# Expert stage laid out anew: 8 KB weight rows into four banks, the second matrix one job behind, low halves over the raw part, row tables ahead of the loop

## The reference

```
h = RMSNorm(x);  logits = h @ w_router + b_router
gate = softmax(top 4 of logits)
gu  = h_rows @ w_gu[e] + b_gu[e]                     # 1024 -> 2048 (gate | linear)
g   = min(gu[:, :1024], 7);  l = clip(gu[:, 1024:], -7, 7)
act = g * sigmoid(1.702 * g) * (l + 1)
y   = act @ w_down[e] + b_down[e]                    # 1024 -> 1024
x[token] += gate * y      for each of the token's four experts
```

## Time and profile before

| | us |
|---|---|
| median of 3 runs | 1790.51 (1790.03 to 1791.18) |
| the profiled execution, its own time | 1789.55 |
| its span, first to last instruction | 1787.7 |
| PE busy, whole span | 1642.5 (92%) |
| DVE busy | 1384.4 (77%) |
| ACT busy | 1089.3 (61%) |
| POOL busy | 235.4 (13%) |
| mean granted PE clock | 0.98 |

### The profile page before, as it was taken

How to read it: one execution, slowest core, us unless ns; L and a number is a source line. 1 busy time by engine, 2 the same in 40 slices (tenths; PEclk the granted TensorE clock), 3 DMA queues, 4 the chain that set the end, 5 groups by cost and what they waited for, 6 DMA issues and landing times.

```text
span 1787.7 us, 23152 instructions
## 1 busy us (share of the span) xinstructions
PE 1642.5 (92%) x7877; PEld 1203.5 (67%) x7877; DVE 1384.4 (77%) x1531; ACT 1089.3 (61%) x1073; POOL 235.4 (13%) x194
## 2 busy tenths in 40 slices
PE   5999999999679999999999999999999999899994
PEld 4877788888556666666666666666666666666662
DVE  5656642426588789898988989888888989888895
ACT  5356742324265677667667766766677676767764
POOL 7300000000001112111111111111111111111120
PEclk9999999999789999999999999999999999999997
DMA  8310012337199999999999999999999999999994
GB/s 263 105 62 19 1 37 87 122 108 260 69 329 339 340 309 341 352 342 344 342 345 326 340 341 343 342 329 346 335 319 341 346 339 347 347 348 323 339 341 135
DMA packets 202066, 480.13 MB, mean 269 GB/s; under 512 B 10976, under 2 KB 11504, under 8 KB 201904
## 3 DMA queue, kind: packets, MB, share of 16 engines
q1 hardware_dynamic: 193824, 452.36, 70.0%
q0 software_dynamic: 7888, 27.23, 7.7%
q10 hardware_dynamic: 320, 0.08, 0.0%
HBM read 460.86 MB, written 19.66 MB: 269 GB/s over the span
## 4 chain that ended last, share of the span: by engine, by line
PE 58%; DVE 18%; issue 15%; ACT 6%; DMA 2%; DVEq 0%; ACTq 0%; SPq 0%; POOLq 0%; POOL 0%
PE ps L1300 16%; PE ps L1302 16%; PE ps L1301 16%; DVE w_low L1074 10%; ACT w_high L762 3%; PE ps L1325 3%; PE ps L1419 2%; DVE act_sb L1256 2%; PE ps L1393 1%; DVE at_lo L1235 1%; DVE sg_sb L1279 1%; DVE g_sb L1251 1%; PE ps L1549 1%; ACT y_sb L836 1%; PE ps L1384 1%
## 5 line engine op out<-in xcount | busy, mean ns | idle before, releaser
L1074 DVE TENSOR_TENSOR w_low<-w_raw,w_high 128x2048 fp32r<-128x2048 f32 x388 | 876.5, 2283 | 131.6 <-ACT w_high L762 131.5
L762 ACT ACTIVATE w_high<-w_raw 128x2048 fp32r<-128x2048 f32 x388 | 719.8, 1903 | 20.2 <-PE ps L1302 10.5
L1300 PE MATMUL ps<-w_high,xt_hi 128*96 128x512 f32 x1024 | 427.4, 417 | 5.3 <-DVE xt_lo L1235 5.3
L1302 PE MATMUL ps<-w_high,xt_lo 128*96 128x512 f32 x1024 | 404.9, 395 | 0.0
L1301 PE MATMUL ps<-w_low,xt_hi 128*96 128x512 f32 x1024 | 402.8, 393 | 0.0
L1300 PE MATMUL ps<-w_high,at_hi 128*96 128x512 f32 x512 | 216.2, 422 | 69.8 <-DVE at_lo L1235 69.8
L1300 PEld LDWEIGHTS ps<-w_high,xt_hi 128*96 128x96 f32 x1024 | 165.9, 162 | 75.0 <-DVE w_low L1074 5.9
L1301 PEld LDWEIGHTS ps<-w_low,xt_hi 128*96 128x96 f32 x1024 | 166.2, 162 | 71.3
L1302 PEld LDWEIGHTS ps<-w_high,xt_lo 128*96 128x96 f32 x1024 | 165.4, 161 | 71.6
L886 POOL TENSOR_TENSOR mark_sb<-ones 1x1 f32<-1x1 f32 x64 | 71.8, 1122 | 1072.4 <-ACT y_sb L836 830.2
L1302 PE MATMUL ps<-w_high,at_lo 128*96 128x512 f32 x512 | 204.2, 399 | 0.0
(11 more groups left out here) (227 smaller groups left out, 1895.5 us busy)
## 6 DMA issues: line engine op xcount, KB each, us to landing
w_raw<-in_w_gate_up SPq DMA_DIRECT2D x260, 1024.0 KB, 7.0
w_raw<-in_w_down SPq DMA_DIRECT2D x128, 1024.0 KB, 6.5
w_raw<-in_w_in SPq DMA_DIRECT2D x8, 2048.0 KB, 9.2
w_raw<-in_w_out SPq DMA_DIRECT2D x2, 2048.0 KB, 8.1
x_sb<-in_x SPq DMA_DIRECT2D x4, 512.0 KB, 6.3
w_raw<-in_w_in SPq DMA_DIRECT2D x2, 1024.0 KB, 17.0
w_raw<-in_w_mem_kv SPq DMA_DIRECT2D x1, 2048.0 KB, 14.6
x<-in_x SPq DMA_DIRECT2D x4, 512.0 KB, 5.2
```

Of the source, the lines that this page charges most:

```text
L762: nc.scalar.activation(half_of(wh, m, SPLIT_SLOTS), half_of(raw, m, RAW_SLOTS), ACT.Copy).then_inc(wh_done, 1)
L1074: nc.vector.tensor_tensor(half_of(wl, m, SPLIT_SLOTS), half_of(raw, m, RAW_SLOTS), half_of(wh, m, SPLIT_SLOTS).bitcast(F32), ALU.subtract) ...
L1300: nc.tensor.matmul(bank, hi, w_hi, start=start, stop=False)
L1302: return nc.tensor.matmul(bank, lo, w_hi, start=False, stop=stop)
```

## The change

In the expert stage nearly all is laid out anew; attention and router stay.

- A part of the gate and linear matrix is now 128 whole rows of 8 KB (one k for all four banks), a part of the down matrix two times 128 rows of 4 KB as before. PE runs each k over banks 0 to 3: high by high, low by high, then high by low.
- Order of jobs: gate_up(0), then in the loop gate_up(j+1), down(j); after the loop the last gate_up and two downs. The activations span 1024 columns at once and go through ACT's Relu and Sigmoid: with r = Relu(7 - g), Sigmoid(1.702 * 7 - 1.702 * r) is the sigmoid of 1.702 * min(g, 7). Transposes of the activations come after the second part of the next gate_up, transposes of tokens after the first part of a down.
- Memory: twelve raw slots of 8 KB, eight slots for high halves; the low half is written over its raw part. ACT runs eight parts ahead, DVE seven. SP waits for PE's part twelve back instead of DVE's.
- All rows, gates and experts of all jobs are worked out in tables ahead of the loop; POOL and ACT copy a job's column from them. The per-job selection on DVE and PE goes.
- The bias operand is made by ACT, the transposes of a whole activation are taken as 768 columns at once.

```
 # SP
-                    for p in range(PARTS):
-                        load_part(e, i, 2 * PARTS + b * PARTS + p)
+                    for k in range(KD):
+                        wait_part(sp, i, stream(b, k) - A_SLOTS)
+                        load_gu(e_gu, stream(b, k), k)
+                    for q in range(DN_PARTS):
+                        wait_part(sp, i, stream(b, KD + q) - A_SLOTS)
+                        load_dn(e_dn, stream(b, KD + q), q)
...
 # ACT
+            def moe_high(i, m):
+                wait_raw(act, i, m)
+                if m >= H_SLOTS or not isinstance(i, int):
+                    wait_part(act, i, m - H_SLOTS)
+                nc.scalar.activation(h_w[m % H_SLOTS][:], a_w[m % A_SLOTS][:], ACT.Copy).then_inc(wh_done, 1)
...
+                    for p in range(PARTS):
+                        if p == 2:
+                            take_act(j)
+                        if p == KD - 1:
+                            wait_part(act, i, stream(b, p))
+                            sigmoid(j + 1)
+                        if p == KD + 1:
+                            take_xt(j + 2)
+                        moe_high(i, stream(b, p) + H_LEAD)
...
+                    take_y(j, b)
...
 # DVE, ahead of the loop
+            for t in range(TB):
+                c = slice(t * TOP_K, (t + 1) * TOP_K)
+                step.inc(nc.vector.tensor_tensor(job_hots[:, c, :], numbers(NJ), spread(dest_jobf[:, c], NJ), ALU.is_equal))
+                step.inc(nc.vector.tensor_tensor(slot_hot[:, c, :], numbers(SLOTS), spread(dest_slot[:, c], SLOTS), ALU.is_equal))
+                dve.wait_ge(dve_chain, step.n)
+                step.inc(nc.vector.tensor_tensor(job_vals[:, c, 0, :], job_hots[:, c, :], spread(dest_vals[:, c, 0], NJ), ALU.mult))
+                nc.vector.tensor_tensor(job_vals[:, c, 1, :], job_hots[:, c, :], spread(dest_vals[:, c, 1], NJ), ALU.mult).then_inc(vals_ready, 1)
...
 # DVE, in the loop
+                        if p == 2:
+                            low_act(j)
+                        if p == KD - 1:
+                            wait_part(dve, i, stream(b, p))
+                            clamp(j + 1)
+                        if p == KD + 1:
+                            low_xt(j + 2)
+                        moe_low(i, stream(b, p) + LOW_LEAD)
+                        if p == KD - 1:
+                            activate(j + 1)
...
 # PE
+            def gate_up(i, j, m0, between):
+
+                pe.wait_ge(expert_gu_ready, j + 1)
+                for n in range(4):
+                    nc.tensor.matmul(ps[0:SLOTS, n, :], expert_gu[:], bias_gu[:, n * COLS:(n + 1) * COLS], start=True, stop=False)
+                pe.wait_ge(xt_lo_done, j + 1)
+                for k in range(KD):
+                    m = m0 + k
+                    w_h, w_l = h_w[m % H_SLOTS], l_w[m % A_SLOTS]
+                    wait_high(pe, i, m)
+                    for x_part in (xt_hi, xt_lo):
+                        for n in range(4):
+                            nc.tensor.matmul(ps[0:SLOTS, n, :], x_part[:, k, :], w_h[:, n * COLS:(n + 1) * COLS], start=False, stop=False)
+                    wait_low(pe, i, m)
+                    for n in range(4):
+                        last = nc.tensor.matmul(ps[0:SLOTS, n, :], xt_hi[:, k, :], w_l[:, n * COLS:(n + 1) * COLS], start=False, stop=k == KD - 1)
+                    last.then_inc(gemm_ps, 1)
+                    between(k)
...
+                    pe.wait_ge(gs_ready, j + 1)
+                    pe.wait_ge(l_ready, j + 1)
+                    gate_up(i, j + 1, stream(b, 0), last_act)
+                    down(i, j, stream(b, KD), next_tokens)
...
+            gate_up(pairs_but_one, j + 1, stream(0, 0), last_act_but_one)
+            down(pairs_but_one, j, stream(0, KD), last_act_of_all)
+            down(pairs_but_one, j + 1, stream(0, PARTS), lambda q: None)
```

More of the change, by code:

```diff
@@ new lines, in encoder_kernel @@
+        xt_hi = sb("xt_hi", [P, KD, SLOTS], F32R, 160 * KIB)
+        xt_lo = sb("xt_lo", [P, KD, SLOTS], F32R, 163 * KIB)
+        xg = [sb(f"xg{i}", [SLOTS, D], F32, (166 + 4 * i) * KIB) for i in range(2)]
+        at_hi = sb("at_hi", [P, KD, SLOTS], F32R, 174 * KIB)
+        at_lo = sb("at_lo", [P, KD, SLOTS], F32R, 177 * KIB)
+        sg_sb = sb("sg_sb", [SLOTS, D], F32, 180 * KIB)
+        act_sb = sb("act_sb", [SLOTS, D], F32, 184 * KIB)
+        y_sb = sb("y_sb", [SLOTS, D], F32, 188 * KIB)
@@ L792, in _ @@
                     take_h2(t - 1)
-            for m in range(3, LEAD):
-                moe_high(0, m)
+            moe_high(0, 3)
             take_h2(TB - 1)
@@ new lines, in take_act, with sigmoid @@
+            def take_act(j):
+                act.wait_ge(at_ps, j + 1)
+                nc.scalar.activation(at_hi[:].rearrange("p (h k) m -> p h (k m)", h=2), of_two_banks(6), ACT.Copy).then_inc(at_hi_done, 1)
+            def sigmoid(j):
+                nc.scalar.activation(sg_sb[:].rearrange("p (h n) -> p h n", h=2), ps[0:SLOTS, 0:2, :], ACT.Relu, bias=limits[0:SLOTS, 0:1],
+                                     scale=-1.0).then_inc(under_limit, 1)
+                act.wait_ge(under_limit, j + 1)
+                nc.scalar.activation(sg_sb[:], sg_sb[:], ACT.Sigmoid, bias=limits[0:SLOTS, 1:2], scale=-ALPHA).then_inc(sg_ready, 1)
@@ new lines, in keep_gate, with take_y @@
+            def keep_gate(j, b):
+                nc.scalar.activation(y_gate[:, b:b + 1], slot_gates[:, bass.ds(j, 1)], ACT.Copy).then_inc(gate_kept, 1)
+            def take_y(j, b):
+                act.wait_ge(gate_kept, j + 1)
+                act.wait_ge(added, j * 16 + 16)
+                nc.scalar.activation(y_sb[:].rearrange("p (h n) -> p h n", h=2), ps[0:SLOTS, 4:6, :], ACT.Copy,
+                                     scale=y_gate[:, b:b + 1]).then_inc(y_ready, 1)
+            for m in (4, 5):
+                moe_high(0, m)
@@ new lines, in _ @@
+            act.wait_ge(table_ready, 1)
+            act.wait_ge(slots_ready, 1)
+            act.wait_ge(hot_b_ready, 1)
+            act.wait_ge(limits_ready, 1)
+            nc.scalar.activation(mark_act[:], ones[0:1, 0:1], ACT.Copy).then_inc(y_ready, 1)
+            name_gu(0)
+            for m in (6, 7):
+                moe_high(0, m)
+            take_xt(0)
+            for p in range(KD):
+                if p == 1:
+                    name_gu(1)
+                if p == KD - 1:
+                    wait_part(act, 0, KD - 1)
+                    sigmoid(0)
+                moe_high(0, p + H_LEAD)
@@ L915, in _ @@
-            pool.wait_ge(added, n_pairs * 32 + 16)
-            for s in range(2):
-                pool.wait_ge(xg_in[s], n_pairs * 16 + 16 * (1 - s))
+                    pool.wait_ge(x_ps, j + 2)
+                    mark(j * 3 + 2)
+                    keep_row(gather_row[:, 1 - b:2 - b], j + 3)
+                    keep_row(sum_row[:, b:b + 1], j)
+                    pool.wait_ge(rows_kept, j * 2 + 5)
+                    mark(j * 3 + 3)
+                    gather(1 - b)
+                    scatter(j, b)
@@ L919, in _ @@
+            for b in range(2):
+                j = pairs_but_one * 2 + b
+                mark(j * 3 + 2)
+                keep_row(sum_row[:, b:b + 1], j)
+                pool.wait_ge(rows_kept, pairs_but_one * 4 + 4 + b)
+                mark(j * 3 + 3)
+                scatter(j, b)
+            pool.wait_ge(added, pairs_but_one * 32 + 48)
+            pool.wait_ge(xg_in[0], pairs_but_one * 16 + 32)
         @block.vector
```

577 lines of the change are left out of this document (278 added, 299 removed).

## The result

The changed kernel takes 1692.3 us, median of 4 runs (1691.29 to 1694.15), against 1790.53 for the kernel before on the same chip: a ratio of 0.9452, interval 0.9441 to 0.9464. The profiled execution took 1692.21 us with a span of 1690.4. The forecast was 1705 with 1686 to 1743 around it. The direction, the mechanism and the bound are as forecast; it came out 13 us faster.

What follows compares the result with a forecast made beforehand. PE with one latency gap a job was taken as the bound, DMA close behind. 501 + 2.2 + 32 x 36.4 + 5.3 + 2.8 + 3.5 + 24.1 = 1703.7, with 1.85 around it 1705.5, stated as 1705; range 1686 to 1743.

Steps and rivals of the forecast that it cites:

- The bound: Kernel before: PE, busy 94%, with one stall of 2.7 or 1.7 us per job ahead of `at_lo` products; DMA close behind.
- PE's work per job: Expert jobs after the change: 36.4 us each, low end 36.1, against 39.2 before; 2.2 stall and 0.6 selection saved.
- the two sums: PE's job after the change: 36.1 us from itemised products, 36.4 from the pair of jobs less stalls and selection; 36.4 taken.
- DVE and ACT: Expert jobs: DVE needs 32.8 and ACT 31.7 of 36.4 us, both fit; the 6 us activation chain is hidden.
- DMA: Weight loads, gather and scatter per job: 19.8 + 10.2 + 4.7 = 34.7 us, 1.7 under PE; 8 KB rows at 423 GB/s.
- rival 1: Expert jobs: DMA becomes the bound, 8 KB rows no faster than 2 KB rows; 29 us more, 1734; chance 0.21.
- Start: Expert stage's beginning: rows ready 489.7, gather 490.4, tokens 497.4, first product 501 (ends 499 and 506), 2.5 us later than before.
- Fill, drain and clock: Edges of the expert loop: 5.3 us wait after gate_up(0), clock losses 2.2 and 2.8, 3.5 at the last down.
- the four terms: Extras beyond the jobs: 2.2 start clock, 5.3 fill gap, 2.8 clock after it, 3.5 drain; 13.8 us.
- A new wait in lock step: Expert jobs: ACT, DVE and PE waits bring half the stall back, 38.0 us a job, 1756; chance 0.12.
- Contiguous megabytes read badly: Gate_up loads as unbroken 1 MB blocks run slower; at 300 GB/s 42.9 us a job, 1913; chance 0.04.
- Dearer products on rotation: PE's products slow by 0.02 us each when banks rotate, 2.9 us a job, 1797; chance 0.03.

Runs made afterwards that it cites:

- Experiment 9: Kernel before with only the second activation halves moved one weight part earlier on ACT and DVE: 1715.8 us, ratio 0.9583.
- experiments 3 and 4: Changed kernel with only high-by-high products and low halves of 256 columns; 3 has 8 KB rows, 1597.33 us; 4 has gate_up in 2 KB rows, 1644.3 us.
- experiment 8: Changed kernel with four unused selection products of 4 columns added to each job's gate_up: 1713.37 us, interval 36.55.
- experiment 1: Changed kernel with gate_up weights read again in 2 KB rows, products bank by bank: 1698.26 us, ratio 0.948.
- experiment 2: Changed kernel without the offset, down(j) directly after gate_up(j): 2005.57 us.
- Experiment 6: Changed kernel with ninth and later weight loads held until the first gather lands, low halves 1 and 2 until POOL copied two gathers' rows: 1683.71 us, ratio 0.9409.

## Why the prediction was right, step by step

**The bound: right.** PE had one latency gap a job and little else. Experiment 9 shows it from the side of the kernel before, and experiments 3 and 4 show that DMA was not the bound, in either kernel. The reading that decided it was ACT's 0.1 us of idle time in 306 instructions, none of it for a DMA.

**PE's work per job: right, 0.5 too high.** Forecast 36.4 with 36.1 as the low end, measured 35.89. That is 32 x 0.51 = 16.3 us, more than the whole miss. The step that was mis-sized is the choice between the two sums: what I couldn't itemise went away as well. Taken from start to start with waits left out, PE's work without the selection was indeed 36.4 in the kernel before. The 48 products of a down matrix fell from 11.62 to 11.35 us, the eight transpose records of the tokens from 0.77 to 0.61; why the first got cheaper was not tested. The rotation over four banks, priced between 0 and 0.02 us per product more, cost nothing (23.09 us for gate_up, 23.11 in experiment 9). The gain of 3.3 us a job (39.2 less 35.89) divides so:

| part | us per job | shown by |
|---|---|---|
| stall ahead of `at_hi` products | 2.1 (39.2 to 37.1) | experiment 9 |
| selection products | 0.66 | experiment 8 |
| down products cheaper (11.61 to 11.35) | 0.26 | traces of experiment 9 and after; cause not tested |
| stall that is left in experiment 9 | 0.23 | its trace, PE's wait for `at_lo` |
| gate_up products (23.11 to 23.09) | 0.02 | the same traces |
| transposes | 0.05 | the same traces; cause not tested |
| DMA rows of 8 KB | 0 | experiments 1, 3, 4: need 35.2 to 33.7, off the path |

The stall was measured in the kernel before and the selection in the changed one, so the sum takes them as independent, which no run shows.

**DVE and ACT: right.** DVE is busy 0.90 of the time (32.8 / 36.4 = 0.90 forecast), ACT 0.78, which is 27.9 us a job where I had 31.7: the 2.6 us of table loads were wrong, the loop has none now. The activation chain is hidden; experiment 2 uncovers it at 5.97 us, forecast 6, with a wrong term in it (see there).

**DMA: right in its order, about 1 us too high.** 34.7 forecast and 33.7 measured with 8 KB rows, 36.6 and 35.2 with 2 KB rows. The error is in the reading of share 0.98 as 0.98/1.05 of need: gather and scatter take less than the 4.7 that this left for them; with the same row prices the measured 33.7 leaves 33.7 - 20.0 - 10.2 = 3.5. The rate of the 8 KB rows was hit (423 and 420). The rule of the Trainium skill (DMA: Bandwidth & Descriptors, section Where 436 GB/s comes from) that the HBM side binds at some 358 GB/s per core, weighed with rival 1, does not hold for this one core: it had 396 GB/s for 900 us in experiment 3.

**Start: the step with the largest error against me.** First product at 505.69, forecast 501, ends 499 and 506. The row tables were ready at 488.8, 0.9 earlier than forecast, the gather was issued at 491.43, 1.0 later, and the tokens were turned at 502.28, 4.9 later. Two things were missed, both at POOL. `gather_row` took 2.34 us beside a low half that DVE started at 488.82, 0.01 us after it. And the gather took 10.9 us from its issue to the tokens' transposes, not 7.0, beside the four loads that SP issued from 491.90 on. The 7.0 was itself misread: in the kernel before the gather landed 4.2 us after its issue, with no weight load in flight, and PE came to the tokens only after other work, its idle time ended by "issue" and not by the gather. Experiment 6 removes both and gets 8.5 us, 9.3 in the time. The first matches a rule of the Trainium skill (SBUF — State Buffer, section 🔬 SBUF: two separate sides): GpSimd and DVE share a port pair as an exclusive lock, and a DVE operation with two SBUF inputs holds it against a GpSimd operation that reads SBUF. By that rule the copy ends with the low half, at 491.11; the trace has it end at 491.15. The page says that whichever starts first gets the ports; the trace writes the copy's start 0.01 us ahead, so it doesn't settle who had them.

**Fill, drain and clock: right.** PE's stretch is 505.69 to 1666.69 = 1161.0, which is 32 x 35.89 = 1148.5 and 12.5 of extras; the four terms made 13.8. The gap was 4.79 (5.3 forecast). The drain was 2.24 at `take_y` instead of 2.5, and the 1 us for its transposes didn't come. The tail is 1690.4 - 1666.7 = 23.7 (24.1).

**The sum.** +4.7 for the start, -16.3 for the jobs, -1.3 for the extras, -0.4 for the tail: -13.3, from 1703.7 to 1690.4, the measured span.

**The rivals.** DMA as the bound: no, and in experiment 1 not even with the old rows. A new wait in lock step: no, PE has no idle time from 600 to 1600. Contiguous megabytes read badly: no, 420 GB/s. Dearer products on rotation: no, 0.2315 us each.

## What to carry to other kernels

A resource at a share near 1 isn't the bound until somebody waits for it: look for an engine that waits for a DMA, and measure the need by making the other engines light. With an engine at 94%, look at what ends its few gaps first; here one operation queued behind two long ones cost 2 us in 39, and moving it up past one of them was 4.2% without any new layout. Once a stage is bound by one engine all through, what is left lies in its edges: here 16 us in the first gather, the fill, the drain and the clock in them.

## What the runs showed of the hardware

- A GpSimd copy of 96 numbers took 2.34 us beside a DVE subtraction of 128x2048 and 0.20 without it. The issue of an indirect DMA took 2.73 us against 0.99 for the gather and 3.43 against 1.44 for the scatter. It is what runs beside them that counts: in experiment 2 no low half runs when the scatter's issue begins, and it takes 1.44 in the changed layout too; in experiment 6 the first gather's issue takes 0.99 with no low half beside it and the second 2.85 beside two.
- The first gather of 96 rows landed 4.1 us after its issue in experiment 6 and 4.2 in the kernel before, both with no weight load in flight, and 10.7 in the changed kernel beside four megabytes.
- One core streamed 396 GB/s over 900 us with 8 KB and 4 KB rows mixed, and 379 with 2 KB and 4 KB rows; 420 in 6 us of 8 KB rows alone. The DMA share reads up to 1.05, so 0.98 isn't full.
- In the expert stage the granted clock went to its lower level (1.2 GHz) only behind PE idle time, and not behind each of its waits: in the kernel before three times after 600 us, where nearly every job had a stall of 1.7 or 2.7. Products on data that nobody reads kept it at 2.4 GHz through waits of 5 us and more. With 19 of them at the fill, and PE idle for 1.32 and 1.13 us behind them, it read 0.73 over the next stretch (527 to 530); with 24 and the second wait gone too, it stayed at 1.00.
